# Value projections in groups of four tiles across head borders, head loops written out

## The reference

```python
h = einsum('bsd,de->bse', x, w_in)        # 2048 -> 3*3072 + 1024 + 1024 + 1024 + 4096 columns
q, k, v, z_attn, u_pool, z_pool, g_pre = split(h)
# q, k, v: 3 groups x 8 heads x 128; per group a causal dilated window (128,1), (512,4), (2048,16)
# scores = q k / sqrt(128), masked; softmax over the three groups together; o = probs v
y_attn = o * silu(z_attn)                                  # 8 heads x 128
y_pool = (per-group map of (trailing mean of u_pool - u_pool)) * pool_scale * silu(z_pool)
g_attn, g_pool = split(sigmoid(g_pre + b_gate))
merged = g_attn * (y_attn @ w_proj_attn) + g_pool * (y_pool @ w_proj_pool)
out    = merged @ w_out
return layer_norm(2**0.25 * x + out, ln_gamma, ln_beta)
```

## Time and profile before

| | |
|---|---|
| median of 3 runs | 943.57 us (943.24 to 943.77) |
| the profiled execution | 943.51 us |
| its span in the profile | 941.7 us |
| granted TensorE clock, mean | 0.998 |
| PE busy | 934.0 us (99%), 5382 matmuls |
| PEld busy | 836.5 us (89%) |
| DVE busy | 635.8 us (68%) |
| ACT busy | 420.8 us (45%) |
| DMA | 178.30 MB, mean 189 GB/s |

### The profile page before, as it was taken

How to read it: one execution, slowest core, us unless ns; L and a number is a source line. 1 busy time by engine, 2 the same in 40 slices (tenths; PEclk the granted TensorE clock), 3 DMA queues, 4 the chain that set the end, 5 groups by cost and what they waited for, 6 DMA issues and landing times.

```text
span 941.7 us, 14853 instructions
## 1 busy us (share of the span) xinstructions
PE 934.0 (99%) x5382; PEld 836.5 (89%) x5382; DVE 635.8 (68%) x1004; ACT 420.8 (45%) x585; POOL 0.2 (0%) x4
## 2 busy tenths in 40 slices
PE   9999999999999999999999999999999999999997
PEld 7998998998998998998998999888888888888886
DVE  7667567567567567567567567666666666666866
ACT  7354354354354354354354354545445444444340
POOL 0000000000000000000000000000000000000000
PEclk9999999999999999999999999999999999999999
DMA  9745545545545545545545545655555554557432
GB/s 374 259 156 182 196 160 182 193 161 181 193 160 181 191 163 179 193 163 178 190 166 179 189 169 223 223 184 209 187 178 188 185 206 178 186 204 281 178 134 90
DMA packets 26541, 178.30 MB, mean 189 GB/s; under 512 B 3343, under 2 KB 3855, under 8 KB 5903
## 3 DMA queue, kind: packets, MB, share of 16 engines
q1 hardware_dynamic: 26064, 173.72, 51.3%
q10 hardware_dynamic: 452, 4.24, 1.1%
HBM read 175.85 MB, written 2.10 MB: 189 GB/s over the span
## 4 chain that ended last, share of the span: by engine, by line
PE 99%; DVE 1%; issue 0%; DVEq 0%
PE proj_ps L364 39%; PE proj_ps L368 20%; PE attn_ps L364 7%; PE attn_ps L356 4%; PE attn_ps L358 4%; PE attn_ps L357 4%; PE attn_ps L368 3%; PE value_ps L358 3%; PE value_ps L356 3%; PE value_ps L357 3%; PE mixed_ps L358 1%; PE mixed_ps L356 1%; PE mixed_ps L357 1%; PE mixed_ps L494 1%; PE proj_ps L401 1%; PE attn_ps L431 1%
## 5 line engine op out<-in xcount | busy, mean ns | idle before, releaser
L364 PE MATMUL proj_ps<-xt,w_hi 128*128 128x512 f32 x1600 | 557.1, 392 | 0.0
L368 PE MATMUL proj_ps<-xt,w_lo 128*128 128x256 f32 x1600 | 446.9, 279 | 0.0
L788 DVE TENSOR_TENSOR w_lo<-w_raw,w_hi 128x1024 fp32r<-128x1024 f32 x314 | 369.3, 1220 | 71.0 <-ACT w_hi L632 69.4
L364 PEld LDWEIGHTS proj_ps<-xt,w_hi 128*128 128x128 f32 x1600 | 299.5, 187 | 66.5
L632 ACT ACTIVATE w_hi<-w_raw 128x1024 fp32r<-128x1024 f32 x314 | 314.2, 1051 | 44.0 <-PE mixed_ps L358 25.1
L368 PEld LDWEIGHTS proj_ps<-xt,w_lo 128*128 128x128 f32 x1600 | 301.9, 189 | 0.0
L652 ACT ACTIVATE corr<-proj_ps 128x256 f32<-128x256 f32 x102 | 39.1, 383 | 280.4 <-PE proj_ps L368 278.8
L802 DVE TENSOR_TENSOR qk_f<-proj_ps,corr 128x256 f32<-128x256 f32 x46 | 19.5, 424 | 76.1 <-ACT corr L652 76.1
L364 PE MATMUL attn_ps<-yp,w_hi 128*128 128x512 f32 x128 | 45.1, 391 | 0.0
L364 PE MATMUL attn_ps<-ya,w_hi 128*128 128x512 f32 x128 | 45.1, 391 | 0.0
L358 PE MATMUL value_ps<-w_hi,xt 128*128 128x384 f32 x128 | 42.9, 335 | 0.0
(11 more groups left out here) (178 smaller groups left out, 957.2 us busy)
## 6 DMA issues: line engine op xcount, KB each, us to landing
w_raw<-in_weights SPq DMA_DIRECT2D x158, 1024.0 KB, 4.8
first_raw<-in_first SPq DMA_DIRECT2D x8, 640.0 KB, 8.1
res<-in_x_rows ACTq DMA_DIRECT2D x1, 2048.0 KB
out_rows<-res SPq DMA_DIRECT2D x7, 256.0 KB, 2.5
gamma<-in_gamma_row ACTq DMA_DIRECT2D x1, 1024.0 KB
beta<-in_beta_row ACTq DMA_DIRECT2D x1, 1024.0 KB
mask<-in_mask SPq DMA_DIRECT2D x1, 512.0 KB, 18.1
out_rows<-res SPq DMA_DIRECT2D x2, 128.0 KB, 2.9
```

The lines of the kernel that those rows point to most:

```text
L364: mm(bank, w_hi[:, slot, k * P:(k + 1) * P], tile.rearrange("p a s -> p (a s)"), start=first, stop=False)
L368: done = mm(bank[:, SEQ:2 * SEQ], w_lo[:, slot, k * P:(k + 1) * P], tile[:, 0, :], start=False, stop=last)
L788: tt(w_lo[:, slot, cols], w_raw[:, slot, cols], w_hi[:, slot, cols].bitcast(F32), ALU.subtract).then_inc(lo_split, 1)
```

## The change

Values are computed in six groups of four tiles (512 columns) instead of eight of three (384). The 24 value tiles are numbered head by head; group n holds tiles 4n to 4n + 3, so it crosses head borders, and lies in four chunks instead of three. Heads 0, 1, 2, 4, 5 and 6 have 13 chunks (j = 6 to 9 are values), heads 3 and 7 have 9 and no value chunk: their z_attn, u_pool and z_pool are j = 6, 7, 8. `v_hi` and `v_lo` grow to a ring of six tiles. In heads 3 and 7 the splitting of pt moves behind szp, to j = 0 of the next head (or, for head 7, behind its last chunk), and the mix of head 3 comes after chunk 0 of head 4. The loop over heads is written out on all three engines. `pool_map` takes its groups in the order 2, 3, 0, 1, and waits for head 7's pt split before group 0, whose bank holds pt.

At the beginning, pieces 1 and 2 are split chunk by chunk like piece 0 (`BY_CHUNK = 3`), and chunks 3 to 5 of head 0 take two k-tiles together (`FIRST_TOGETHER = 2`: two matmuls of 512, then two of 256). At the end, the last block is stored in one piece (`LAST_PARTS` is gone). The rest follows from these: `banked` and `bank_of` count the chunks that use a bank, by a table.

```diff
+BY_CHUNK = 3
-A_STEPS, A_CHUNKS = HEADS, 12
...
+QK, V_GROUP, V_CHUNKS, V_TILES = 2 * GROUPS, 4, 4, 6
+A_BANKED = QK + 3
+def groups_by(h):
+    return -(-GROUPS * (h + 1) // V_GROUP)
+def has_values(h):
+    return groups_by(h) > groups_by(h - 1)
+def a_chunks(h):
+    return A_BANKED + V_CHUNKS * has_values(h)
+START = [sum(a_chunks(h) for h in range(before)) for before in range(A_STEPS + 1)]
...
+MAP_ORDER = (2, 3, 0, 1)
+def value_runs(group):
+    first = group * V_GROUP % V_TILES
+    fits = min(V_GROUP, V_TILES - first)
+    runs = [(0, first, fits)] + ([(fits, 0, V_GROUP - fits)] if fits < V_GROUP else [])
+    return [tuple(P * tile for tile in run) for run in runs]
-A_TOGETHER, B_TOGETHER = 1, 1
+FIRST_TOGETHER, A_TOGETHER, B_TOGETHER = 2, 1, 1
...
-                    ("v_hi", [TT, GROUPS * P], F32R),
-                    ("v_lo", [TT, GROUPS * P], F32R), ("mask", [TT, KEYS], F32),
+                    ("v_hi", [TT, V_TILES * P], F32R),
+                    ("v_lo", [TT, V_TILES * P], F32R), ("mask", [TT, KEYS], F32),
...
-            return [slice(n, n + 1) for n in range(ABREAST)] if q == 0 else [slice(0, ABREAST)]
+            return [slice(n, n + 1) for n in range(ABREAST)] if q < BY_CHUNK else [slice(0, ABREAST)]
...
+            def values(c, i):
+                group, n = groups_by(i) - 1, START[i] + QK + c
+                if c == 0:
+                    pe.wait_ge(v_split, FROM + VALUE_PARTS[group])
+                for kk in range(BLOCK_KT):
+                    k, cols = c * BLOCK_KT + kk, slice(kk * BLOCK, (kk + 1) * BLOCK)
+                    if kk % 2 == 0:
+                        pe.wait_ge(lo_split, 2 * n + kk // 2 + 1)
                     for t in range(TT):
                         tokens = slice(t * P, (t + 1) * P)
                         done = product(v_ps[t][:, :], xt[:, k, 0, tokens], xt[:, k, 1, tokens],
-                                       ring_hi[:, cols], ring_lo[:, cols], k == 0, k == KT - 1)
-                    if j > 0 and k == before:
-                        done.then_inc(chunk_done, 1)
-                if j == GROUPS - 1:
-                    done.then_inc(chunk_done, 1)
+                                       w_hi[:, n % RING, cols], w_lo[:, n % RING, cols], k == 0, k == KT - 1)
+                done.then_inc(chunk_done, 1)
...
-                pe.wait_ge(v_split, FROM + i * TT + TT)
+                pe.wait_ge(v_split, FROM + VALUE_PARTS[groups_by(i)])
...
+                pe.wait_ge(v_split, FROM + VALUE_PARTS[-1])
                 slot = POOL_MAP % RING
-                for g in range(POOL_TILES // 2):
+                for g in MAP_ORDER:
+                    if g == 0:
+                        pe.wait_ge(pt_split, FROM + A_STEPS * PT_BANKS)
...
-                        chunk(0, j, i, A_CHUNKS, from_x(j % 2))
+                        chunk(n, 0, 0, 0, from_x(bank_of(n, 0)), FIRST_TOGETHER if first and j < QK else A_TOGETHER)
...
                     if j == PT_AFTER:
                         turn_probs(i)
-            head(0, True)
-            mix(0)
-            with pe.Fori(1, A_STEPS - 1) as i:
-                head(i, False)
-                mix(i)
-            head(A_STEPS - 1, False)
+                    if j == 0 and i > 0 and not has_values(i - 1):
+                        mix(i - 1)
+            for i in range(A_STEPS):
+                head(i, i == 0)
+                if has_values(i):
+                    mix(i)
...
+            def pt_hi_parts(i):
+                for b in range(PT_BANKS):
+                    act.wait_ge(pt_ready, i * PT_BANKS + b + 1)
+                    activation(pt[:, b, 0, :], attn_ps[:, b * 512:(b + 1) * 512],
+                               ACT.Copy).then_inc(pt_hi_done, 1)
...
-            head(0, True)
-            mix_correction(0)
-            with act.Fori(1, A_STEPS - 1) as i:
-                head(i, False)
-                mix_correction(i)
-            head(A_STEPS - 1, False)
+            for i in range(A_STEPS):
+                head(i, i == 0)
+                if has_values(i):
+                    mix_correction(i)
...
+            def pt_lo_parts(i):
+                for b in range(PT_BANKS):
+                    dve.wait_ge(pt_hi_done, i * PT_BANKS + b + 1)
+                    tt(pt[:, b, 1, :], attn_ps[:, b * 512:(b + 1) * 512],
+                       pt[:, b, 0, :].bitcast(F32), ALU.subtract).then_inc(pt_split, 1)
...
-            with dve.Fori(1, A_STEPS - 1) as i:
-                chain.i = i
-                head(i, False)
-                gated_mix(i)
-            assert chain.count - start_a == per_a, chain.count - start_a
-            chain.count, chain.i = start_a, A_STEPS - 1
-            head(A_STEPS - 1, False)
+            for i in range(A_STEPS):
+                head(i, i == 0)
+                if has_values(i):
...
-                for cols in (slice(c * BLOCK, (c + 1) * BLOCK),) if c < BLOCKS - 1 else LAST_PARTS:
-                    at = res[:, t, cols]
-                    stt(out=at, in0=at, scalar=rstd[:, 2 + t:3 + t],
-                        in1=norm_shift(c)[:, cols.start - c * BLOCK:cols.stop - c * BLOCK],
-                        op0=ALU.mult, op1=ALU.add).then_inc(out_ready, 1)
+                at = res[:, t, c * BLOCK:(c + 1) * BLOCK]
+                stt(out=at, in0=at, scalar=rstd[:, 2 + t:3 + t], in1=norm_shift(c)[:, :],
```

More of the change, by code:

```diff
@@ L75 @@
 BLOCKS = D_MODEL // BLOCK
-LAST_PARTS = tuple(slice(c, c + BLOCK // 2) for c in range(D_MODEL - BLOCK, D_MODEL, BLOCK // 2))
 BLOCK_CHUNKS = OT // BLOCKS
@@ L81 @@
 FROM = 1
-V_FIRST, Z_ATTN, U_POOL, Z_POOL = 6, 9, 10, 11
 SCORES_AFTER, SOFTMAX_SUM, PT_AFTER, PT_SPLIT = 6, 7, 8, 9
-assert V_FIRST % RING == 0 and GROUPS == RING
+VALUE_PARTS = [TT * sum(len(value_runs(g)) for g in range(before)) for before in range(groups_by(A_STEPS - 1) + 1)]
 KEYS = SEQ + (GROUPS - 1) * P
@@ L517, in pool_map @@
                                            first=(kk == 0), last=(kk == 1))
-                    last.then_inc(pool_ready if g < POOL_TILES // 2 - 1 else chunk_done, 1)
+                    last.then_inc(pool_ready if g != MAP_ORDER[-1] else chunk_done, 1)
             def head(i, first):
-                for j in range(A_CHUNKS):
+                for j in range(a_chunks(i)):
+                    n = START[i] + j
                     if first and j < ABREAST:
@@ L719, in _ @@
             mix_correction(A_STEPS - 1)
-            for g in range(POOL_TILES // 2):
-                act.wait_ge(yp_f_ready, g + 1)
+            for n, g in enumerate(MAP_ORDER):
+                act.wait_ge(yp_f_ready, n + 1)
                 activation(yp[:, 2 * g:2 * g + 2, 0, :],
@@ L889, in split, with v_lo_parts @@
                 tt(both[:, 1, :], src, both[:, 0, :].bitcast(F32), ALU.subtract).then_inc(signal, 1)
-            per_a = 28
-            start_a = chain.count
+            def pt_lo_parts(i):
[3 more added lines that the diff above has]
+                       pt[:, b, 0, :].bitcast(F32), ALU.subtract).then_inc(pt_split, 1)
+            def v_lo_parts(i):
+                group = groups_by(i) - 1
+                runs = value_runs(group)
+                for t in range(TT):
+                    dve.wait_ge(v_hi_done, VALUE_PARTS[group] + (t + 1) * len(runs))
+                    for source, dst, width in runs:
+                        tt(v_lo[:, t, dst:dst + width], v_ps[t][:, source:source + width],
+                           v_hi[:, t, dst:dst + width].bitcast(F32), ALU.subtract).then_inc(v_split, 1)
             def head(i, first):
-                for j in range(A_CHUNKS):
+                z_attn = z_attn_at(i)
+                for j in range(a_chunks(i)):
+                    n = START[i] + j
                     if j == SOFTMAX_SUM:
@@ L940, in head @@
                                       op0=ALU.mult, op1=ALU.mult))
+                    if j == 0 and i > 0 and not has_values(i - 1):
+                        gated_mix(i - 1)
             def gated_mix(i):
@@ L1171, in _stream @@
         order = [part * qkv + g * HEADS + h for g in range(GROUPS) for part in range(2)]
-        order += [None] * GROUPS + [z_attn + h, u_pool + h, z_pool + h]
+        order += [None] * (a_chunks(h) - A_BANKED) + [z_attn + h, u_pool + h, z_pool + h]
         for j, tile in enumerate(order):
@@ L1175, in _stream @@
                 stream[n + j] = cols[tile].reshape(P, CHUNK)
-        values = cols[2 * qkv + h:3 * qkv:HEADS].transpose(1, 2, 0, 3).reshape(P, GROUPS, CHUNK)
-        stream[n + V_FIRST:n + V_FIRST + GROUPS] = values.transpose(1, 0, 2)
-        n += A_CHUNKS
+        if has_values(h):
+            group = range(V_GROUP * (groups_by(h) - 1), V_GROUP * groups_by(h))
+            values = cols[[2 * qkv + tile % GROUPS * HEADS + tile // GROUPS for tile in group]]
+            values = values.transpose(1, 2, 0, 3).reshape(P, V_CHUNKS, CHUNK)
+            stream[n + QK:n + QK + V_CHUNKS] = values.transpose(1, 0, 2)
+        n += a_chunks(h)
```

166 lines of the change are left out of this document (79 added, 87 removed).

## The result

The changed kernel takes **950.12 us** in the median of 7 runs (948.11 to 955.27), the kernel before 943.27 beside it (943.15 to 943.77): ratio 1.0087, 95% interval 1.0068 to 1.0106. It is slower, by 6.9 us, and lies outside the range of the prediction. Thirteen executions of it, the last experiment's six among them, fall on three levels and nowhere between: 948.1 to 948.4 (five), 950.0 to 950.3 (four), 954.9 to 955.3 (four). The kernel before has one level. A median of such a kernel depends on how often each level came up; the time that can be compared without luck is the lowest, 948.1. The profiled execution is on the highest: 955.27 us, span 953.5, so 11.8 above the span before.

What follows compares the result with a forecast made beforehand. TensorE was taken to bound the kernel, on the chain for 99% of the span. The terms -2.9 - 0.2 + 0.15 + 2.9 + 0.2 - 0.2 came to -0.1 unrounded, giving 943.4 us, range 940.9 to 945.4.

Steps and rivals of the forecast that it cites:

- values: Value matmuls on TensorE: 576 of 512 columns at 226.8 ns, 192 matmuls fewer, 133.5 to 130.6 us: -2.9 us.
- head loops written out: Loop over heads on TensorE: the back edge costs nothing now, and written-out heads 1 to 7 keep their pace: 0.
- FIRST_TOGETHER: Chunks 3 to 5 of head 0, two 512s then two 256s: between nothing and 0.3 us gained, taken as -0.2.
- finer splits: Pieces 1 and 2 at the start: extra VectorE split work can move its end, -0.1 to +0.3, taken as +0.15 us.
- head 7's waits: Pool map after head 7: TensorE waits 0.4 and 2.4 us on VectorE's splits, +2.9 us, bounds 1.9 and 3.5.
- head 3's wait: Mix of head 3, after the next head's chunk 0: ready at 24.63 against 24.80, +0.2 us, bounds 0 and 0.8.
- last stores: End of kernel: one 256 KB store for two of 128 KB, between -0.6 and +0.2, taken as -0.2 us.
- Rival (a): Written-out projection chunks of heads 1 to 6 run at head 0's pace: 5.7 us more, 949.1 us, slower; chance 0.06.
- rival (c): Value stage: extra time belongs to columns, not matmuls, so it keeps its 133.5 us; some 946 us, slower; chance 0.02.
- Rival (b): Wait before pool group 0 is hidden, TensorE loses under 1 us in head 7: 940.5 us, faster; chance 0.14.

Runs made afterwards that it cites:

- the last experiment: The changed kernel itself, unaltered, run six more times to see how often each level comes up: 949.23 us median.
- e1: The kernel before with only its three loops over heads 1 to 6 written out: 942.8 us against 943.59, ratio 0.9992.
- e10: The kernel of e8 with only the first piece split chunk by chunk, as in the kernel before (BY_CHUNK = 1): 941.13 us.
- e9: The kernel of e8 with the last block stored in two halves of 128 KB, as in the kernel before: 940.69 us.
- e3: The changed kernel with head 7's two pt splits put ahead of the pool's last splits on ACT and DVE: 946.04 us.
- e8: The changed kernel with z_attn's matmuls in pairs in heads with values and head 7's pt splits early: 940.73 us against 943.59, ratio 0.9970.
- e7: The changed kernel with z_attn's matmuls in pairs (two 512, two 256) in each head that computes values: 942.90 us.

## Why the prediction was wrong

| step | predicted, us | measured, us |
|---|---|---|
| values | -2.9 | -2.1 (133.5 to 131.4) |
| head loops written out | 0 | -0.8 (e1, medians; +0.4 at the start and -0.76 at the end in the traces) |
| FIRST_TOGETHER | -0.2 | -0.24 (16.96 to 16.72) |
| finer splits | +0.15 | about -0.4 (e10) |
| head 7's waits | +2.9 | +2.7 (0.35 ahead of the map, 8.08 - 5.74 in it) |
| head 3's wait | +0.2 | 0 |
| last stores | -0.2 | 0 by the medians, -0.3 by means and traces (e9) |
| slow rhythm in stage A | not in the sum | +5.4 |
| half clock behind the wait | not in the sum | +1.5 in the map, 1.9 between levels, in 8 of 13 executions by their levels |
| slow rhythm in stage B | not in the sum | +5.1 in 4 of 13 by their levels |

**The step that failed** is the one under "Head loops written out": "I take 0 for heads 1 to 7". The row that decided was on the table: the earlier trace rows show the same matmuls at 176.7 ns in head 0 and at 173.4 in head 2. I asked only whether the slower pace belongs to code without a loop, found against it that stage C is written out and isn't slow, and costed it at nothing. That argument was sound as far as it went (e1), and the text even named what fits better, "a pattern that the next small matmuls reset"; but I didn't follow it. If the pace is a matter of what ran before, then a change that alters what runs before, and value matmuls of another width do that, puts every projection matmul of heads 1 to 7 at stake, 7 x 9 x 32 = 2,016. The bound from the earlier trace rows was 3.3 ns by that number, 6.7 us, against a whole sum of 0.1. The size in stage A is 33.92 - 33.29 = 0.63 for each of heads 1, 2, 5 and 6, 0.74 for the seven chunks of 3 and 7, and 16.95 - 16.72 = 0.23 behind the values of six heads: 5.4 us. The second step that failed is under "Heads 3 and 7": the wait before pool group 0 was priced at its own length, and nothing was put on what it does to the matmuls behind it, which was up to 6.9 us (the levels of 948.2 and 955.1).

**Rival (a)** named 949.1 us, close to the median, at a chance of 0.06, and its row in "what would show it wrong", chunks written out at 176 ns, came true in the trace. Its mechanism did not: e1 has the loops written out, and the projections of heads 1 to 7 open at 173.4. That its 5.7 us are close to the 5.4 of stage A, and its time close to the median, is luck.

**Head 7** came out as worked out. The prediction had 5.32 us from the pool tile's arrival to the last pt split, and the map's start and its group 0 are 579.88 - 574.76 = 5.12 apart; the wait is 2.0 where it said 2.4, and the head 7 term as a whole 2.7 where it said 2.9, inside the bounds of 1.9 and 3.5. What it left out is what a standing TensorE does to the work behind it. The kernel before had no wait of this kind after the beginning, so no row of it showed a fall of the clock in the middle. Its trace has one at the end, where TensorE is done (the granted clock is the 0.50):

```profile
937.90:941.70 3.80, 0.00 (x0) 0.50 0.66 194
```

So a clock that falls when TensorE stands could be seen beforehand, though not what it would cost here, and a longer range upwards would have followed.

**The values** gained 2.1 and not 2.9. At 226.8 ns, as in stage C, 576 would take 130.6 us; those behind the turns take 231.3 ns (135.69 to 141.24, 24 of them), nearly all of it in the first start, which is 0.31 us instead of 0.23, and the others 227.1 to 227.5. The time does go with the number of matmuls, so rival (c) fell: at 2.4 GHz 512 columns are 213.3 ns, and the value matmuls take 13.8 ns on top of it between scores and turns, as those of 384 columns did before (173.8 against 160.0). The Trainium skill's 2.5 ns a matmul ("TensorE: Matmul & The Clock Gate", section "Wait — 56ns, not 53.3ns?") isn't what these matmuls show.

**Rival (b)**, a hidden wait, is what e3 makes by another order of the splits, but the time it gives is 946.0, not 940.5, because of the rhythm; with the rhythm mended too (e8) it is 940.7.

From the first projection matmul to stage B the kernel before and e1 both need 572.8 us, with loops or without. So the Trainium skill's stall at a taken branch ("Runtime: NRT & Kernel Launch", section "Instruction fetch mechanics") isn't seen here; the page ties it to targets outside what has been fetched, which no run here varies.

**Head 3**, the finer splits and the stores were each good to half a microsecond, the finer splits with the wrong sign.

## What to carry over

Where one engine is busy all the time, look at whether the same instruction has two paces in the trace before, and what stands ahead of each; if the change alters what stands ahead, the whole class of instructions belongs in the bound, however small the difference of one. A wait on the bounding engine is not only its own length: ask what follows if the clock falls behind it, and take away a wait of this kind first, since at 2.0 us it made the time scatter as well. When such a change turns out slower, its parts may still be good: with the order of one chunk in each of six heads and two splits moved, this one is 0.3% faster than the kernel before.

## What the runs showed that was not expected

- Alternating matmuls of 512 and 256 columns have two stable rhythms at the full clock, 173.4 and 176.6 ns each. Which one holds is set by what ran before, and lasts through hundreds of microseconds: stage B's 1,536 matmuls stay in either from end to end. In pairs, 512, 512, 256, 256, they ran at 174.2 ns in all of stages A and B, where the other order was fast or slow. What in the engine keeps the rhythm, these runs don't say.
- After TensorE had stood for 2.0 us in the pool map, the clock was at the 1.2 GHz level for some 3.4 us (580.7 to 584.1 by the matmuls' starts), beginning 0.8 us after it had resumed. By the levels of 950 and 955 us this came in eight of thirteen executions of the changed kernel, and by the same signs in three of eleven of e7, which has the same wait. A stand of 1.52 us at the same place, in the kernel before, was never followed by it in 11 executions; one of 2.65 us was not in one execution of six.
- Stores of 128 KB at the end landed in 2.2 us in the programs without loops and in 2.9 to 3.0 in those with them. TensorE's first projection matmul started 0.4 us later without loops.
